# Sparse attention of a transformer block: the rest of the score grid is subtracted on GpSimd, and the row's exponent takes one small VectorE operation

## The reference

```
logits = einsum('bqhc,bqkc->bqhk', qa, c_sel) * (DSA_DH ** -0.5)
logits = where(dist >= 0, logits + bias, -1e30)
p = softmax(logits, axis=-1)
o = einsum('bqhk,bqkc->bqhc', p, c_sel)
```

## Time and profile before

| what | value |
|---|---|
| runs | 3620.32, 3626.01, 3626.83 us (median 3626.01) |
| span of the profiled execution | 3619.8 us, 46994 instructions |
| TensorE busy | 3353.8 us, 93% of the span |
| TensorE weight loads busy | 2652.9 us, 73% |
| VectorE busy | 1792.0 us, 50% |
| ScalarE busy | 1218.3 us, 34% |
| GpSimd busy | 1070.2 us, 30% |
| mean granted TensorE clock | 0.967 of full speed |

### The profile page before, as it was taken

One profiled execution on the slowest core, in us unless ns is written; L12 is line 12 of the kernel. 1 busy time (PEld: TensorE's weight loads), 2 busy tenths in 40 slices (PEclk: granted clock), 3 DMA queues, 4 the chain that ended last, 5 costly groups with the idle time before them and its releaser, 6 DMA issues. The chain is left out here.

```text
span 3619.8 us, 46994 instructions
## 1 busy us (share of the span) xinstructions
PE 3353.8 (93%) x18342; PEld 2652.9 (73%) x18342; DVE 1792.0 (50%) x3378; ACT 1218.3 (34%) x2265; POOL 1070.2 (30%) x589
## 2 busy tenths in 40 slices
PE   7799897799989899999999989999899999998988
PEld 5478675699878777888888867776666677775667
DVE  1788788655554426554544570335444502344443
ACT  3475566444222302000000131334453213344540
POOL 3133000154444335544534333220112332201112
PEclk9899999799999999999999999999999999999999
DMA  3111100000212114221322113110102211101011
GB/s 117 30 41 29 33 5 1 8 1 22 85 53 64 41 35 142 82 93 58 104 70 67 55 41 101 45 36 12 24 1 82 82 55 49 44 13 18 7 71 70
DMA packets 234301, 179.90 MB, mean 50 GB/s; under 512 B 42945, under 2 KB 219249, under 8 KB 233217
## 3 DMA queue, kind: packets, MB, share of 16 engines
q1 hardware_dynamic: 231376, 176.56, 16.0%
q10 hardware_dynamic: 2736, 0.78, 0.1%
HBM read 159.92 MB, written 16.87 MB: 49 GB/s over the span
## 5 line engine op out<-in xcount | busy, mean ns | idle before, releaser
L1102 DVE SCALAR_TENSOR_TENSOR y_T<-y_T 128x1024 f32<-128x1024 f32 x48 | 137.4, 2914 | 0.1
L881 ACT ACTIVATE I-13450a_hi<-I-13449act_f 128x512 fp32r<-128x512 f32 x22 | 13.5, 633 | 338.5 <-DVE I-13449act_f L890 338.5
L914 DVE TENSOR_TENSOR x_T<-x_T,I-13456p_d 128x512 f32<-128x512 f32 x88 | 60.3, 687 | 126.3 <-PE I-13456p_d L846 126.3
L283 PE MATMUL I-13454p_g<-hf_hi,I-13430w_hi 128*128 128x512 f32 x352 | 108.8, 390 | 3.4 <-POOL hf_lo L523 3.4
L1688 DVE TENSOR_TENSOR I-22508S<-I-22508S,c_causal 128x256 f32<-128x256 f32 x32 | 13.8, 431 | 198.1 <-PE I-22508S L1615 198.1
L283 PE MATMUL I-13455p_u<-hf_hi,I-13431w_hi 128*128 128x512 f32 x352 | 109.0, 391 | 2.3 <-POOL I-13433w_lo L269 2.3
L285 PE MATMUL I-13455p_u<-hf_lo,I-13431w_hi 128*128 128x512 f32 x352 | 109.2, 392 | 0.0
L1688 DVE TENSOR_TENSOR I-16194S<-I-16194S,c_causal 128x256 f32<-128x256 f32 x32 | 13.8, 431 | 192.0 <-PE I-16194S L1615 192.0
L287 PE MATMUL I-13455p_u<-hf_hi,I-13433w_lo 128*128 128x512 f32 x352 | 108.8, 390 | 0.0
L285 PE MATMUL I-13454p_g<-hf_lo,I-13430w_hi 128*128 128x512 f32 x352 | 108.4, 389 | 0.0
L287 PE MATMUL I-13454p_g<-hf_hi,I-13432w_lo 128*128 128x512 f32 x352 | 108.4, 389 | 0.0
(11 more groups left out here) (1390 smaller groups left out, 10176.0 us busy)
## 6 DMA issues: line engine op xcount, KB each, us to landing
y_T<-in_w_ada SPq DMA_DIRECT2D x48, 512.0 KB, 3.5
saved_x<-x_T SPq DMA_DIRECT2D x3, 4096.0 KB, 13.6
I-13428w_raw<-in_w_gate SPq DMA_DIRECT2D x22, 512.0 KB, 4.5
I-13429w_raw<-in_w_up SPq DMA_DIRECT2D x22, 512.0 KB, 4.1
x_T<-saved_x SPq DMA_DIRECT2D x2, 4096.0 KB, 14.5
I-13442d_raw<-in_w_down SPq DMA_DIRECT2D x11, 512.0 KB, 4.9
I-13443d_raw<-in_w_down SPq DMA_DIRECT2D x11, 512.0 KB, 4.9
I-895w_raw<-in_w_in SPq DMA_DIRECT2D x8, 512.0 KB, 3.8
```

Of the source, the lines that this page charges most:

```text
L283: nc.tensor.matmul(out[h], w_hi[:, k, :], hi(k, h), start=(k == 0), stop=False)
L881: nc.scalar.activation(a_hi[s][:, cols], act_f[:, cols], ACT.Copy).then_inc(a_rounded, 1)
L914: nc.vector.tensor_tensor(x_n, x_n, p_d[n % 2][:, h, :], ALU.add).then_inc(d_added[n % 2], 1)
L1102: self.nc.vector.scalar_tensor_tensor(out=self.raw[s], in0=self.raw[s], scalar=1.0, in1=self.c_row, op0=ALU.mult, op1=ALU.mult, accum_out= ...
```

## The change

In the stage, the subtraction leaves VectorE and goes to GpSimd, which does it as soon as the grid part of the unit is there (`rest_of`). The two column operations become one, which no longer adds the half step; the half step is now the bias of ScalarE's second exponential, read from a column `half_grid` that GpSimd sets once. The splits of the weights, which GpSimd did in a loop of their own, stand between its subtractions, each after the subtraction of the unit with r == 4.

```diff
+                def rest_of(u):
+                    w, s = unit(u)[3], u % 3
+                    moved, part = probs[s][:, 0:w], grid[s][:, 0:w]
+                    pool.wait_ge(gridded, u + 1)
+                    nc.gpsimd.tensor_tensor(moved, part, moved, ALU.subtract).then_inc(rest_done, 1)
+
+                nc.gpsimd.memset(half_grid[:, :], GRID / 2).then_inc(half_set, 1)
+                split(0)
+                for u in range(UNITS):
+                    rest_of(u)
+                    i, r = divmod(u, 2 * NT)
+                    if r == 4 and i + 1 < PAIRS:
+                        split(i + 1)
...
-                    nc.scalar.activation(rest[:, 0:w], rest[:, 0:w], ACT.Exp).then_inc(exp_done, 1)
+                    nc.scalar.activation(rest[:, 0:w], rest[:, 0:w], ACT.Exp, bias=half_grid[:, 0:1]).then_inc(exp_done, 1)
...
+                act.wait_ge(half_set, 1)
                 exponentials(0)
...
                     v.tensor_scalar(part, moved, GRID_ROUND, GRID_ROUND, ALU.add, ALU.subtract).then_inc(gridded, 1)
-                    v.tensor_scalar(least[:, one], least[:, one], GRID_ROUND, None, ALU.add).then_inc(least_shifted, 1)
-                    dve.wait_ge(least_shifted, u + 1)
-                    v.tensor_scalar(neg[:, one], least[:, one], GRID_ROUND, GRID / 2, ALU.subtract, ALU.add).then_inc(bias_set, 1)
-                    dve.wait_ge(gridded, u + 1)
-                    v.tensor_tensor(moved, part, moved, ALU.subtract).then_inc(rest_done, 1)
+                    v.tensor_scalar(neg[:, one], least[:, one], GRID_ROUND, GRID_ROUND, ALU.add, ALU.subtract).then_inc(bias_set, 1)
```

More of the change, by code:

```diff
@@ L2432, in sparse_stage @@
         latents_turned, latents_out = st.sem("latents_turned"), st.sem("latents_out")
-        scored, reduced, least_shifted, bias_set, gridded = (st.sem(n) for n in ("scored", "reduced", "least_shifted", "bias_set", "gridded"))
+        scored, reduced, bias_set, gridded = (st.sem(n) for n in ("scored", "reduced", "bias_set", "gridded"))
+        half_grid, half_set = st.sb("half_grid", [P, 1]), st.sem("half_set")
         rest_done, exp_done, probs_ready = (st.sem(n) for n in ("rest_done", "exp_done", "probs_ready"))
@@ L2501, in _, with split @@
                 raw, hi, lo = flat(w_raw), flat(w_hi), flat(w_lo)
-                for i in range(PAIRS):
+                def split(i):
                     pool.wait_ge(w_in, 16 * (i + 1))
```

## The result

The changed kernel takes 3636.59 us in the median (3630.86 to 3643.88, 8 runs), beside 3625.59 us for the kernel before (3620.32 to 3631.15, 8 runs): ratio 1.0032, 95% interval 1.0020 to 1.0044, so 0.32% or 11 us slower. Its profiled execution took 3637.2 us with a span of 3634.7.

The account below looks back on a forecast made before the run. TensorE sets the pace, VectorE close behind. Seven heads' delays 5.2, first head 0.8, last units -0.3 and clock falls 3.0 make 8.7 us on 3626.0: 3634.7, say 3635; range 3619 to 3645, the forecast's own 3631 to 3641.

Parts of the forecast that it names:

- The hold: VectorE's multiplications stand until GpSimd's subtraction ends; in first heads T1 0.62, T8 0.68, T7 0.73 us late.
- the turns of the seven heads: TensorE's delay at T7 in the seven later heads: four of 0.73 and three of 0.75, 5.2 us.
- The clock: Longer TensorE waits at heads lower its clock: 1.5 us a fall, 0 to 6 us possible, two falls or 3.0 taken.
- The first head: Start of the stage: first exponential waits 2.40 us for GpSimd instead of about 1.2; 0 to 1.2 us, 0.8 taken.
- A table load of ScalarE hides a little: At the stage's first exponential: the load covers part of the 0 to 1.2 us delay, so 0.8 was taken.
- ScalarE's wait for the half step: Before the first exponential, for GpSimd's memset: done long before, costed at nothing.
- relief in the last five units: End of the stage, no auxiliary work on TensorE, so VectorE's relief counts: 0 to -0.6 us, -0.3 taken.
- GpSimd's durations: GpSimd's subtraction: 2.40 us in the longest hold, 2.12 for 896 columns, 1.83 for 768.
- ScalarE's bias: Half step in ScalarE's second exponential: costed at nothing; if 0.1 us slower each, 6 us mostly beside TensorE's work.
- TensorE's waits: TensorE's waits for VectorE's multiplications in the stage: to rise above 11.8 us, to about 18.
- at least two units later in the order: Place of ScalarE's exponential, said to cover GpSimd's longer subtraction nearly everywhere.
- Rival B: VectorE's multiplication not held or just slowed; about 10 us of TensorE's waits go: 3616 us, chance 0.11.

Follow-up runs that it names:

- run 1: Changed kernel with the subtraction back on VectorE, the single column operation and ScalarE's bias kept: 3624.66 us, ratio 0.9998 to the kernel before.
- run 2: Changed kernel with the two column operations restored and no bias in the exponential, GpSimd still subtracting: 3632.8 us, ratio 1.0023 to the kernel before.
- run 5: As run 4, but GpSimd subtracts other tiles at the same moment and nobody waits for the result: 3622.29 us, ratio 0.9991 to the kernel before.
- run 8: Changed kernel, but GpSimd's subtraction for each head's third unit waits for the second unit's multiplication: 3628.93 us, ratio 1.0013 to the kernel before.
- run 11: Changed kernel, but VectorE subtracts each head's second unit, and GpSimd's third-unit subtraction waits for the second's multiplication: 3623.75 us, ratio 0.9996 to the kernel before.
- run 6: As run 5, but GpSimd copies one tile instead of subtracting two: 3614.9 us in one run.
- run 7: Changed kernel with GpSimd's subtraction split into two instructions of half the columns: 3629.19 us, ratio 1.0016 to the kernel before.
- run 3: Changed kernel with ScalarE's wait for the half step moved to the start of its stage: 3633.0 us in one run.
- run 4: Changed kernel with the subtraction left out on every engine, the second exponential waiting for the grid: 3616.59 us, ratio 0.9978 to the kernel before.

## Why the prediction was right

**The hold** was the step on which all rested, and it came as worked out. Measured from the turn of T2 ahead of them, T1's multiplication ended 0.61 us later than before (0.62 predicted), T8's 0.65 (0.68), T7's 0.71 (0.73); the turns of the seven heads moved by 5.1 us for 5.2. Runs 1 and 2 put the loss on GpSimd's subtraction, and run 5 shows that access alone holds VectorE and costs time. Run 8 takes the hold away from T7 and run 11 from T8 too, and the loss goes with it, in part and then wholly. A page of the Trainium skill, "SBUF — State Buffer", section "Who interferes with whom", states it as a lock that is kept for the whole instruction: against a VectorE operation with two inputs in SBUF when GpSimd's reads SBUF, and against one that uses both of VectorE's ports, which `tensor_scalar` can. The traces agree: the multiplication of run 6 ends 0.94 us behind a mere copy, that of run 7 gets in only between two instructions, and the grid operation took 1.82 us for 0.63.

**The clock**: two falls beyond the first head were taken, two are in the profile, 1.6 us each for 1.5. Which heads it meets was not to be had from the waits: the heads of u = 16, 32, 48 and 56 all have waits of 0.96 and 1.90 us or nearly so, and the clock fell behind two. Nor does the sum of two waits decide, by which the prediction went: at the start of run 1's stage TensorE waited 2.07 and 1.89 us, 3.96 together, and the clock stayed at full, where it had fallen behind 3.33 in the kernel before. In runs 2 and 3, with the same waits, it fell behind one; in runs 8 and 11, where the second wait is 0.79, behind none. The number two was luck within a range of none to four.

**The first head** is the term that was mis-sized. "A table load of ScalarE hides a little" was wrong in this program, and so was to cost ScalarE's wait for the half step at nothing: with this third wait ahead of the first exponential the load stands behind GpSimd, and the first multiplication came 1.8 us late, not 0.8; run 3 gives 1.3 of it back. That the head as a whole cost 0.8 us all the same (1.8 - 1.1) is chance. In the kernel before, the low clock of the earlier trace rows met matmuls that nothing else held up: in run 1, which has no fall there, the third turn comes 1.6 us earlier after the first multiplication. In the changed kernel it lay on TensorE's wait of 4.4 us and on turns that wait for VectorE anyway (0.51 from 390 to 396 us); its third turn is 0.2 us behind run 1's.

**The rest**: relief in the last five units 0.2 us for 0.3, GpSimd's durations 2.36, 2.08 and 1.81 for 2.40, 2.12 and 1.83, ScalarE's bias 5.9 us for 6, and hidden. TensorE's waits 17.8 for 18. The prediction has ScalarE's exponential "at least two units later in the order" than the grid part; by the kernel's order it is one. That was covered all the same: T6's exponentials in the head of u = 16 began 1.4 us later than before, not up to 0.8, and were over at 457.14, ahead of T6's multiplication at 458.21. Of the splits one held VectorE, a T5 for 0.4 us, at no cost. The stage is 9.1 us longer for 8.7; the medians differ by 11.0 us, with an interval of 7 to 16, so the part beyond the stage is not shown to be more than spread.

**Rival B** named 3616 us, which is what run 4 measured, on a premise that was wrong and with a sum that does not come out: it had about 10 us of TensorE's waits go, and in run 4 the waits fell by 5.0 us and the stage by 6.8. Without the hold the change could have been at most 0.2% faster.

## What to carry to other kernels

Moving work from VectorE to GpSimd is not moving it away: while GpSimd's instruction runs, VectorE's multiplication of two SBUF tensors, or its rounding from SBUF to SBUF, stands until it ends. Look at what VectorE does in the 1 to 2.4 us behind the hand-over, and give GpSimd only what falls beside operations that read PSUM or beside units for which nobody waits. And ask first whether the relief needs another engine: here one subtraction put behind the multiplication that TensorE waited for gave, with the small operation, 0.13% (0.02 to 0.24), and the change as it stands cost 0.32% (0.20 to 0.44).

## What the runs showed of the hardware

- The hold works in both directions and by the instruction: two GpSimd halves took 2.81 us for 2 x 1.01 when VectorE got in between (run 7).
- Not everything is held. Beside a subtraction of GpSimd these kept their lengths: copies of 512 columns from PSUM (0.69 us), the masking, which reads PSUM and SBUF (0.55 us for 384 columns, run 7), and operations on one column (0.15 us). The rounding to the grid, SBUF to SBUF, was held: 1.53 us for 0.49 with 640 columns (runs 8 and 11).
- GpSimd's duration depends on the operands: 896 columns take 2.08 us from two tiles into one of them, 1.68 from one tile read twice into another, 0.94 as a copy (runs 5 and 6).
- With three waits ahead of the first exponential the table load started only behind the subtraction, on GpSimd in the changed kernel and on VectorE in run 1; with two it ran beside it (the kernel before, runs 2 and 3).
